# A two-block model on one core: the check for general expert blocks, and these blocks, moved into the middle of the experts

## What is computed

```
        xb, e = args
        hu = xb @ w_up[e] + b_up[e]
        x_glu = jnp.minimum(hu[:, :D_FF], SWIGLU_LIMIT)
        x_lin = jnp.clip(hu[:, D_FF:], -SWIGLU_LIMIT, SWIGLU_LIMIT)
        act = x_glu * jax.nn.sigmoid(SWIGLU_ALPHA * x_glu) * (x_lin + 1.0)
        return act @ w_down[e] + b_down[e]
```

## Time and profile before

| | us |
|---|---|
| median of 3 runs | 2661.85 (2657.67 to 2667.33) |
| profiled execution | 2662.46, its span 2661.3 |
| PE busy | 2433.0 (91%) |
| planned experts | about 590 to 1620 |
| granted TensorE clock, mean | 0.947 |

### The profile page before, as it was taken

How to read it: one execution, slowest core, us unless ns; L and a number is a source line. 1 busy time by engine, 2 the same in 40 slices (tenths; PEclk the granted TensorE clock), 3 DMA queues, 4 the chain that set the end, 5 groups by cost and what they waited for, 6 DMA issues and landing times. The chain is left out here.

```text
span 2661.3 us, 27721 instructions
## 1 busy us (share of the span) xinstructions
PE 2433.0 (91%) x10465; PEld 1174.1 (44%) x10465; DVE 959.1 (36%) x2103; ACT 555.9 (21%) x1286; POOL 212.6 (8%) x381
## 2 busy tenths in 40 slices
PE   5988999959999988799999997989998799999999
PEld 2534586543343333334333334655444444454443
DVE  2666364362121111111211124440666662342371
ACT  1244432010000000000000002211555551210350
POOL 1000353010101000110000002000000000000000
PEclk8988999969999999999999998999889899999889
DMA  9201396529999999998999898100000002021000
GB/s 349 70 32 44 147 347 254 217 86 393 426 425 427 426 426 426 415 410 332 411 414 407 366 427 313 64 28 32 1 1 1 0 1 103 32 95 64 32 1 32
DMA packets 122993, 563.99 MB, mean 212 GB/s; under 512 B 18997, under 2 KB 42990, under 8 KB 95074
## 3 DMA queue, kind: packets, MB, share of 16 engines
q1 hardware_dynamic: 104600, 517.55, 48.4%
q0 software_dynamic: 15360, 39.43, 4.0%
q10 hardware_dynamic: 2890, 5.13, 0.6%
HBM read 535.72 MB, written 26.35 MB: 211 GB/s over the span
## 5 line engine op out<-in xcount | busy, mean ns | idle before, releaser
L218 PE MATMUL ps<-mem,ring 128*128 128x512 f32 (+1 forms) x1056 | 422.8, 560 | 2.6 <-DVE mem L795 1.6
L1844 PE MATMUL ps<-ring,mem 128*32 128x512 f32 (+2 forms) x1680 | 389.3, 615 | 23.8 <-issue 23.8
L218 PE MATMUL ps<-ring,mem 128*128 128x512 f32 (+5 forms) x1136 | 388.3, 498 | 18.3 <-ACT ring L2611 8.5
L218 PEld LDWEIGHTS ps<-mem,ring 128*128 128x128 f32 x1056 | 201.9, 192 | 213.8 <-issue 205.2
L218 PEld LDWEIGHTS ps<-ring,mem 128*128 128x128 f32 x1136 | 198.7, 194 | 192.6 <-issue 159.4
L224 PE MATMUL ps<-mem 128*128 128x128 f32 (+2 forms) x1155 | 194.1, 302 | 55.5 <-PEq L2263 10.2
L1844 PEld LDWEIGHTS ps<-ring,mem 128*32 128x32 f32 (+2 forms) x1680 | 134.2, 136 | 239.8 <-issue 237.9
L224 PEld LDWEIGHTS ps<-mem 128*128 128x128 f32 (+2 forms) x1155 | 149.1, 166 | 180.1 <-issue 114.1
L1844 PE MATMUL ps<-mem 128*32 128x512 f32 (+2 forms) x752 | 198.2, 607 | 5.1 <-issue 5.1
L1909 PE MATMUL ps<-mem 128*32 128x512 f32 (+2 forms) x672 | 176.4, 594 | 3.9 <-issue 2.2
L1909 PE MATMUL ps<-ring,mem 128*32 128x512 f32 (+2 forms) x736 | 169.3, 594 | 7.1 <-issue 7.1
(11 more groups left out here) (385 smaller groups left out, 2421.4 us busy)
## 6 DMA issues: line engine op xcount, KB each, us to landing
ring<-in_w_up SPq DMA_DIRECT2D x75, 2048.0 KB, 19.1
mem<-in_w_up SPq DMA_DIRECT2D x37, 2048.0 KB, 21.4
ring<-in_w_down SPq DMA_DIRECT2D x33, 2048.0 KB, 25.4
mem<-in_w_down SPq DMA_DIRECT2D x31, 2048.0 KB, 24.3
ring<-in_w_up SPq DMA_DIRECT2D x56, 512.0 KB, 12.5
ring<-in_w_ada SPq DMA_DIRECT2D x12, 2048.0 KB, 8.5
ring<-in_mod_w SPq DMA_DIRECT2D x8, 2048.0 KB, 11.9
ring<-in_cd_w_in SPq DMA_DIRECT2D x6, 2048.0 KB, 7.8
```

What stands on the lines that cost most here:

```text
L218: i = e.matmul(o, l, r, start=(start and n == 0), stop=(stop and n == len(pairs) - 1))
L1844: m = e.matmul(PS[n][c0:c0 + rows, :], XGT[:, u, k * 128 + c0:k * 128 + c0 + rows], wt[:, kk, n * 512:n * 512 + 512], start=False, stop=(k ...
```

## The change

The body with the check moves from behind the last planned block to between down 8 and up 10 (`SPLIT` = 9). `pe_experts` and its three likes become generators that stop there, and are run on behind the block. A `Lane` now carries its buffers, and the general blocks get such as are free at that point: halves of `XG`, `XGT` and `Y`, and one place for biases in place of six. Their weights go through the two places that were loaded last (`borrowed`) in place of four; if a general block ran, SP loads the two tiles again behind the last one (`give_back`), and PE waits for them. Waits that make this safe are inside the bodies, which a count of zero skips. SP no longer waits for `meet()` ahead of the check. The `meet()` behind the last planned block stays, and the next stage follows it at once.

```diff
+SPLIT = 9
...
         for what, i in expert_steps():
+            if (what, i) == ("up", SPLIT + 1):
+                yield
...
         for i in range(NMAIN):
+            if i == SPLIT + 1:
+                yield
             if i + 2 < NMAIN:
                 pool_gather(e, main, i + 2, blocks[i + 2].col)
...
-    pe_experts(nc.tensor)
-    dve_experts(nc.vector)
-    act_experts(nc.scalar)
-    pool_experts(nc.gpsimd)
-    load_on(nc.sync, n_first + 3)
-    all_stored = [(main.stored[p], 16 * ((NMAIN - p) // 2)) for p in range(2)] + [dlast.at(16)]
-    meet()
...
+    experts = [pe_experts(nc.tensor), dve_experts(nc.vector), act_experts(nc.scalar), pool_experts(nc.gpsimd)]
+    for half in experts:
+        next(half)
+    load_on(nc.sync, n_first)
+    assert all(blocks[SPLIT + d].half is None for d in (-1, 0, 1))
+    borrowed = [issued[0] - 1, issued[0] - 2]
+    early, late = (SPLIT - 1) % 2, SPLIT % 2
...
+    more = Lane("x", [Y[:, late, :]] * 2, [XGT[:, late, :]] * 2, Y[:, late, :], ACTT, [Y[:, early, :]] * 2,
+                [XG[:, early, 0:512].bitcast(BF16)])
...
     def sp_extras(e):
-        for f in finished:
-            e.wait_ge(*f.now())
         def step(j):
+            if j == 0:
+                for n in borrowed:
+                    e.wait_ge(*landed[n])
...
+        def give_back():
+            for n in borrowed:
+                for dst, src in expert_load(e, *tile_of[n]):
+                    e.dma_start(dst(slot(slot_of(n))), src).then_inc(loaded_again.sem, 16)
...
+    for half in experts:
+        for _ in half:
+            pass
+    load_on(nc.sync, n_first + 3)
+    all_stored = [(main.stored[p], 16 * ((NMAIN - p) // 2)) for p in range(2)] + [dlast.at(16)]
+    meet()
     next_stage()
```

More of the change, by code:

```diff
@@ L1831, in pe_up @@
             for c0, rows, x in [(c, r, x) for c0, rows, x, tile in parts for c, r in tiles(c0, rows)]:
-                bias_product(e, PS[n], x, n, 0, c0, rows)
+                bias_product(e, L, PS[n], x, n, 0, c0, rows)
         for q in range(4):
@@ L1856, in pe_up_half @@
             for g in range(2):
-                bias_product(e, PS[2 * g + b], x, 2 * g + h, 0, c0, rows)
+                bias_product(e, L, PS[2 * g + b], x, 2 * g + h, 0, c0, rows)
         for kh in range(2):
@@ L2162, in emit, with borrowed_slot @@
     next_stage()
-    pe_experts(nc.tensor)
-    dve_experts(nc.vector)
-    act_experts(nc.scalar)
-    pool_experts(nc.gpsimd)
-    load_on(nc.sync, n_first + 3)
-    all_stored = [(main.stored[p], 16 * ((NMAIN - p) // 2)) for p in range(2)] + [dlast.at(16)]
-    meet()
-    more = Lane("x")
-    loaded_x = [sem(f"ring_loaded_x{s}") for s in range(4)]
+    experts = [pe_experts(nc.tensor), dve_experts(nc.vector), act_experts(nc.scalar), pool_experts(nc.gpsimd)]
[7 more added lines that the diff above has]
+                [XG[:, early, 0:512].bitcast(BF16)])
+    loaded_x = [sem(f"ring_loaded_x{s}") for s in range(2)]
+    loaded_again = count("ring_loaded_again")
+    for n in borrowed:
+        loaded_again.n += 16 * len(loads[n])
+    def borrowed_slot(m):
+        return slot(slot_of(borrowed[m % 2]))
     def x_parts(j):
@@ L2184, in extra_end, with each_extra @@
     def extra_end(e, j):
[L2186 to L2192, removed]
+        e.wait_ge(more.stored[j % 2], 16 * (j // 2 + 1))
+    def each_extra(e, step, last=None):
         cnt = extra_count(e)
@@ L2200, in behind @@
                     extra_end(e, j)
+                    if last:
+                        last()
                 if j + 1 < NXB:
@@ L2213, in step @@
             pe_down(e, more, j, x_parts(j))
-        each_extra(e, step)
+        each_extra(e, step, lambda: e.wait_ge(*loaded_again.now()))
     def dve_extras(e):
@@ L2229, in step @@
             if j == 0:
-                for t in all_stored:
-                    e.wait_ge(*t)
+                e.wait_ge(main.stored[early], 16 * ((SPLIT - 1) // 2 + 1))
             act_gate(e, more, j)
@@ L2239, in step @@
             ex = e.value_load(XE[0:1, j:j + 1], min_val=0, max_val=NEXP - 1)
+            if j == 0:
+                e.wait_ge(main.stored[late], 16 * (SPLIT // 2))
+                e.wait_ge(main.x_turned, 2 * (SPLIT + 2))
             pool_gather(e, more, j, NMAIN + j)
-            pool_biases(e, more, j, BIASD[bass.ds(ex, 1)].rearrange("a k n -> (a k) n"), j - NBU if j >= NBU else None)
+            pool_biases(e, more, j, BIASD[bass.ds(ex, 1)].rearrange("a k n -> (a k) n"), None)
             pool_store(e, more, j, NMAIN + j)
```

63 lines of the change are left out of this document (38 added, 25 removed).

## The result

| kernel | median us | lowest to highest | ratio to before (95%) | profiled execution: span us, granted clock |
|---|---|---|---|---|
| before (measured again beside it) | 2662.41 | 2657.67 to 4179.48, 19 runs | 1 | 2661.3, 0.947 |
| after | 2671.01 | 2664.84 to 2699.06, 19 runs | 1.0031 (1.0016 to 1.0047) | 2671.7, 0.945 |

The change costs 8.6 us, just over 0.3%, with an interval from 4 to 13 us. One execution of before took 4179.48 us, for which there is no trace; the other 18 lie between 2657.67 and 2672.5 us. The two profiled executions differ by 10.4 us in span, and the marks along PE's timeline place 9.1 of them.

What follows compares the result with a forecast made beforehand. The experts were taken as bound by DMA up to about 1140 us and by TensorE behind it. 2662.5 + 0.6 (end) + 9.5 (middle) = 2672.6, against the median 2672; range for 8 in 10: 2661 to 2681.

Steps and rivals of the forecast that it cites:

- POOL is last and its drain waits for its transfers: Barrier behind down 8: GpSimd's drain lasts until its bias transfers land; PE restarts at 1088.4, 25.5 us after 1062.9.
- 2.8 us behind the landing: Barrier behind down 8: GpSimd's drain ends 2.8 us after the last bias transfer lands at 1085.2.
- rival 1: Behind down 8: drain does not wait or biases land early; restart 1078.4, middle -0.5, 2660 to 2664; chance 0.15.
- The half clock behind the gap: After PE's restart behind down 8: 8.2 us of work at half clock, +4.1 us.
- The cover of 20.1 us: From 1062.9 to 1138.4 us: 15.0 of weight waits and 5.1 of slow product groups fall away for a late PE.
- The middle: Check behind down 8: 25.5 + 4.1 - 20.1 = +9.5 us, range 0 to +14.
- DMA pausing, priced at nothing: Behind down 8: places come free late, DMA pauses a few us, tiles still arrive in time; otherwise 2 to 5 us.
- Not given back later: Behind 1140 us: the one 2.6 us weight wait moves along with PE, so none of the middle's cost returns.
- The end, +0.6: End of the experts: -1.9 us from an earlier turn, +2.5 for half clock; range -2.2 to +2.2.
- Rivals 3 and 4: End gains 8.1 us whole; 3: middle hidden, 2654, chance 0.06; 4: middle as forecast, 2664, chance 0.09.
- rival 2: Behind down 8: skip longer amid weight traffic; two successive fetches, restart 1093, middle +14, 2677 to 2683; chance 0.15.

Runs made afterwards that it cites:

- the kernel with a gap of 17.5 us: Changed kernel, drain kept, but GpSimd fetches the biases that follow block 8 behind the check: 2660.71 us, ratio 0.9995.
- the late load: Changed kernel with biases behind the check, and SP issuing the next stage's third weight tile only after the last expert store landed: 2657.84 us, ratio 0.9977.

## Why the prediction was right

The time was forecast as 2672 and is 2671.0; the sign is right, and the shape of the sum too. By its steps:

- **POOL is last and its drain waits for its transfers: right.** PE restarted at 1089.9 instead of 1088.4. The 1.5 us are the term "2.8 us behind the landing", mis-sized by 1.6: the drain ended 4.4 us behind the last landing here, 4.1 and 4.0 in the two kernels with SPLIT 9 and the biases moved. (The landing came 0.4 us sooner, release and first product took 0.3 us more.) Without the drain the gap was 13.95 us, so rival 1 had the price of the other case within 1.6 us, but not the case.
- **The half clock behind the gap: mis-sized.** It was taken as 4.1 us from 8.2 us of work behind a wait of 10.24; it measured 2.6 us (5.3 us of work) behind a longer one, and 2.2 and 2.9 behind the gaps of 17.5 and 19.0. A longer idle time did not make it dearer. The row itself was worth less, too: from PE's first product behind the experts to the end of its context products are 30.7 us in before, which begin at the half clock, and 27.3 us in after, which begin at the full one: 3.4 us.
- **The cover of 20.1 us: right.** After has no weight wait left, and the kernel with a gap of 17.5 us shows the break-even at 19.7. The middle came to +9.5 as forecast; the two misses above (26.9 for 25.5, 2.6 for 4.1) cancel, so that its agreement to 0.1 us is partly luck.
- **DMA pausing, priced at nothing: right here**, but for a reason that I had only half. DMA was idle for some 5.5 us in 1090 to 1140 (share 0.89, and 0.06 from 1095.9 to 1100.2) and PE never noticed, because it stood 9.5 us late. Behind down 7 the same kind of pause cost 6.5 us.
- **Not given back later: right**, +9.5 at 1148 and +9.4 at 1629.
- **The end, +0.6: it measured -0.3.** The store sets the gathers and the gathers set the turn, as forecast (the first gather 9.9 us behind the last product, 10.6 forecast); turn -2.5 instead of -1.9, and +2.2 instead of +2.5 from there to the long group, most of it the half clock; together -0.3. With the check left out altogether the time is that of before. Rivals 3 and 4, which give the 8.1 us in full, fall with it.
- **The skip amid weight traffic (rival 2): no.** PE's compare took 6.16 us with DMA at a share of 1.01, where it took 6.43 in before at 0.87. The Trainium skill (Advanced Engine Details and Errata, Control Flow Timing) has about 108 ns for a compare-and-branch; here PE's row is 57 times as long, and DVE, SP and POOL took nearly as much (5.9, 5.9 and 5.7 us from compare to drain). ACT alone took 0.5 us, in every kernel with the check in the middle, where it had taken 6.4 us at the end in before; why is open.

What the forecast missed is not in its sum: the step that cost everything, POOL's eight bias transfers ahead of a barrier that drains, could be moved by one statement, and then the change costs nothing. It gains nothing that the times can tell either (0.9995, from 0.998 to 1.001): only with the late load is the kernel 0.2% faster.

## What to carry to other kernels

A barrier in the middle of a stream costs what the last engine brings, and for GpSimd that was the landing of its own transfers and some 4 us more, so issue nothing ahead of a draining barrier that isn't needed by then. A stall is free only up to two bounds at once: PE's later waits in the stretch that is bound by DMA (20 us here), and the loads in flight that keep DMA busy meanwhile; behind that stretch it is paid in full. And look at what is issued just ahead of a small transfer that a chain hangs on: here one 2 MB load made the store wait 5 us, though holding it back gave only 2 to 3 us, because it then ran beside the gathers.

## What I had not expected of the hardware

- A store of one block issued 1.1 us behind a 2 MB load took 7.4 to 8.6 us to land (seven kernels), and 2.9 us in all three with the load held back; a load of constants (320 KB) beside it took 8.2 to 9.2 us in the six of them with the check moved or left out, and 3.3 with the load held back. That the traffic was in its way was known from the bias transfers; that one load alone did it was not.
- The drain of GpSimd ends 4.0 to 4.4 us behind the landing of its last transfer in this place (three kernels). In before I had read 2.8 us from a drain elsewhere.
- The price of the half clock behind a long idle time did not grow with the idle time: 2.6 us behind 26.9, 2.2 behind 13.95 and 17.5, 2.9 behind 19.0, 2.7 behind 21.8 and 1.7 behind 17.1, and 3.4 behind 10.24, where the work behind it was of another kind (short products with pauses).
